# One weight split, one convolution and one pair of evictions moved inside a hybrid DeltaNet and attention layer

## The chip, the cores and the metric

The kernel runs on one core of a Trainium2 chip. The metric is the device time of one execution in microseconds (us), the median of the runs shown. TensorE is PE in the profile (its weight loads are PEld), VectorE is DVE, ScalarE is ACT, GpSimd is POOL, and SyncE, which issues the DMAs, is SP.

## The reference

One layer of a flow-matching backbone handles 512 latent tokens and 128 context tokens of width 1024 with shared weights. Everything is float32.

```python
h = modulate(rmsnorm(x), shift1, scale1)          # shifts, scales: silu(cond) @ w_ada
u = h @ w_in                                      # q, k, v, z, beta and decay logits, NA q/k/v, gates
qkv = silu(short_conv(qkv, conv_w))               # 3 taps along the tokens
o_dn = gated_delta(l2norm(q), l2norm(k), v, g, beta)   # both directions, 8 heads, chunked
o_na = softmax(q_na @ k_na + bias) @ v_na         # 8 heads, 8 x 16 window plus the context keys
x = x + gate1 * ((sig(gA) * (o_dn @ w_pa) + sig(gB) * (o_na @ w_pb)) @ w_out)
x = x + gate2 * swiglu(modulate(rmsnorm(x), shift2, scale2))
```

## The kernel before

Activations lie feature-major: 1024 features are 8 blocks `k` of 128 partitions, and the 640 tokens lie along the free axis. A PSUM bank holds 512 floats, so a product over 640 tokens goes to two banks as two halves of 320 tokens (`HALVES`). Exact float32 products are made from two rounded parts: an operand is split into `big` (rounded, written by ACT) and `small` (the rest, a subtraction on DVE), and each block takes three products (big by big, big by small, small by big), each in two halves: six matmuls of 128x320. The orders on all five engines are written out by hand; the engines meet only at semaphores (`e.wait_ge`) and at named steps (`Steps`), and each engine works strictly in its written order.

**Opening.** Four groups of `w_ada` columns (`ada_group`, four loads each, the third group into tile WAH, the fourth into wa_last) give the shifts and scales of two feature blocks each. ACT copies each group's sums out, PE turns them (`ada_select`), and DVE makes the gains (`gains(p)`, L2618 to L2623). DVE multiplies the input by the inverse norm (`normed`, L2608), applies the gain (`exact_h`, L2630), ACT rounds it (`round_h`) and DVE subtracts (`small_h`, L2636). In the same stretch DVE splits three weights: `opening_kind("q", 1)`, `opening_kind("k", 2)` and that of the beta and decay logits, `wbas`, all by `opening_small` (L2591). PE goes through pairs of blocks `p`: an ada group, the q product, the select, the k product (L1282), and then `logits_mm` (L1298 and L1300), whose first call waits for the logits' split (`pro_lo` 3).

**Heads.** Eight DeltaNet heads follow, each about 77 us. A head ends with a scan of five steps over the tiles, in both directions at once. In step `s` PE makes `ks` (L1537), DVE makes `r` (L2901), PE makes `y` (L1544), ACT scales it, PE makes `av` (L1555, L1556), and DVE updates the state `S` (L2913, not in steps 0 and 4) and adds the output `o` (L2918). PE puts blocks of dense products between these. On DVE `CONV_AT[s]` names the pieces of the next head's convolution that run in step `s`: the first tuple after `r` and before `S`, the second after `o`. Each of q, k and v has three pieces, 0, 1 and the last (L2685, L2688, L2691), each a pass over 641 columns. In step 4, before `o`, DVE also makes the small part of the next dense weight (`small("6")`, L2784), which PE's products right after the last `av` need. The head ends with normalising `o` (L2942), a turn of it on PE (`turn o`, L1588), and the next head's first products. The last head makes no convolution.

**Attention.** Twenty rounds `j` of two (head, tile) units each are interleaved with 56 blocks `pa_block(n, k)` of `o_dn @ w_pa` (L1604), eight for each of the output groups n = 1 to 7 (group 0 is done before with another form). All groups use the same two PSUM banks, 6 and 7. `pa_evict(n)` on DVE (L2993, two instructions of 320 tokens) multiplies the sums by the gate. The last block of group n-1, the scores of the next round (L1645, L1647) and the first block of group n stand in this order on PE; the first block waits for `pa_out`, which the second instruction of the eviction raises. On DVE the eviction stands behind the two `-max` instructions (L3021) of the round and before the two `P` scalings (L3027, L3030).

After these come `w_pb`, `w_out` and the feed-forward part (L1850), which the diff does not touch.

Of the kernel before, what the change touches and what calls it, by code (L numbers as in the profile page):

```python
# [10 lines left out]
ALU = mybir.AluOpType  # L11
# [5 lines left out]
KD = D // P  # L17
# [141 lines left out]
    return STRIPS[part][SPLIT[part].index(at) + 1] if at in SPLIT[part] else None  # L159


CONV_AT = {0: (("q0",), ("q1",)), 1: (("q",), ("k0",)), 2: (("k1",), ("k",)), 3: (("v0",), ("v1",)), 4: (("v",), ())}


def dve_steps():
# [243 lines left out]
def build(nc, A):  # L409
    top = ExitStack()  # L410
    with top:
# [3 lines left out]
        def sem(name):  # L415
            return top.enter_context(nc.semaphore(name))
# [16 lines left out]
        xT, h_small = sb_rounded("xT", [P, KD, TOK])  # L433
        oT, oT_r = sb_rounded("oT", [P, H, TOK])
        naT, naT_r = sb_rounded("naT", [P, KP, TOK])
        W, W_r = sb_rounded("W", [P, 4, KD, P])
        ps = top.enter_context(nc.psum_tensor("ps", [P, 8, 512], F32))
# [38 lines left out]
        xn_done = sem("xn_done")  # L476
# [73 lines left out]

        ld_pa = [sem(f"ld_pa{i}") for i in range(2)]
        pa_mm = sem("pa_mm")
        pa_read = sem("pa_read")
        pa_out = sem("pa_out")
        oT_hi = sem("oT_hi")
# [51 lines left out]
        start = work.enter_context(ExitStack())  # L607
        xin = sb("xin", [P, NT, D], start)
        xs = sb("xs", [P, KD, TOK], start)
        rows = sb("rows", [P, 2, P], start)  # L610
        sqx = sb("sqx", [P, 2, TOK], start)
        rstd = sb("rstd", [P, TOK], start)
        wba = sb("wba", [P, KD, 4 * H], start)
        wbas = sb("wbas", [P, KD, 2, 4 * H], start, F32R)
# [5 lines left out]
        xn = xinf.rearrange("p (k c) -> p k c", k=KD)  # L620
# [76 lines left out]
        pa_big = sb("pa_big", [P, 2, KD, P], na, F32R)  # L697
# [6 lines left out]
        pa_slot, pa_small = ([w[:, i, :, :] for i in (2, 3)] for w in (W, W_r))  # L704
# [108 lines left out]
        HALVES = ((0, HT), (HT, HT))  # L813
# [413 lines left out]
        def _(e):  # L1227
# [4 lines left out]
            for t in range(NT):  # L1232
                e.wait_ge(ld_x[t], 16)
                for j in range(2):
                    n = 2 * t + j
# [361 lines left out]
            def wait(steps, name):  # L1597
                e.wait_ge(steps.sem, steps.after(name))

            def three(bank, big, small, x_big, x_small, k, k_n):  # L1600

                for i, (w, x) in enumerate(((big, x_big), (big, x_small), (small, x_big))):
                    for b, (a, n) in enumerate(HALVES):
                        m = e.matmul(ps[:, bank + b, 0:n], w[:, k, :], x[:, k, a:a + n], start=k == 0 and i == 0, stop=k == k_n - 1 and i == 2, skip_group_check=True)  # L1604
                return m

            def pa_block(n, k):

                if k == 0:
                    if n:  # L1610
                        e.wait_ge(pa_lo, n)
                    else:
                        e.wait_ge(ld_pa[0], 16)
                    e.wait_ge(pa_out, n)
                if n == 0 and k == KD - 1:
                    e.wait_ge(dve_dn.sem, dve_dn.value(H - 1, "o out"))
                if n == 0:
                    for b, (a, w) in enumerate(HALVES):
                        m = e.matmul(ps[:, 6 + b, 0:w], pa_slot[0][:, k, :], oT[:, k, a:a + w], start=k == 0, stop=k == KD - 1, skip_group_check=True)
                    m.then_inc(pa_read, 1)  # L1620
                else:
                    if n == 1:
                        e.wait_ge(oT_lo, k + 1)
                    m = three(6, pa_big[:, n % 2, :, :], pa_small[n % 2], h_small, oT_r, k, KD)
                    if k == KD - 1:
                        m.then_inc(pa_mm, 1)

            def shared(slot):
# [950 lines left out]
        def _(e):  # L2579
# [8 lines left out]
            def opening_small(w_r, w, big, n):  # L2588

                e.wait_ge(pro_hi, n)  # L2590
                e.tensor_tensor(w_r, w, big, ALU.subtract).then_inc(pro_lo, 1)  # L2591

            def opening_kind(kind, n):

                opening_small(W_r[:, slot[kind], :, :], W[:, slot[kind], :, :], OPENING_BIG[kind], n)
# [6 lines left out]
                e.tensor_scalar(diag[:, t, :], IDN, cols[:, SSQ + t:SSQ + t + 1], None, ALU.mult).then_inc(diag_done, 1)  # L2602
            e.wait_ge(rstd_done, 2)
            e.wait_ge(x_out, 2 * NT)
            def normed(p):

                for k in (2 * p, 2 * p + 1):
                    e.tensor_tensor(xn[:, k, :], xs[:, k, :], rstd[:, :], ALU.mult).then_inc(xn_done, 1)  # L2608

            def gains(p):  # L2610

# [21 lines left out]
            def small_h(k):  # L2633

                e.wait_ge(h_round, k + 1)
                e.tensor_tensor(h_small[:, k, :], xn[:, k, :], h_big[:, k, :], ALU.subtract).then_inc(h_done, 1)  # L2636

            normed(0)
            normed(1)
            e.wait_ge(vec_out, 1)  # L2640
            gains(0)
            exact_h(0)
# [1 line left out]
            small_h(0)  # L2644
            exact_h(1)
            small_h(1)
            opening_kind("k", 2)
            gains(1)
            exact_h(2)
            exact_h(3)  # L2650
            small_h(2)
            small_h(3)
            opening_small(wbas[:, :, 1, :], wba[:, :, :], wbas[:, :, 0, :], 3)
            normed(2)
            normed(3)
            gains(2)
            exact_h(4)
            exact_h(5)
# [326 lines left out]

            def pa_evict(n):
                e.wait_ge(ld_gate[n % 2], 16 * (n // 2 + 1))
                if n:
                    e.wait_ge(pa_mm, n)
                else:  # L2990
                    e.wait_ge(pa_read, KD)
                for b, (a, w) in enumerate(HALVES):
                    m = e.scalar_tensor_tensor(hT[:, n, a:a + w], tA[:, n % 2, a:a + w], 1.0, ps[:, 6 + b, 0:w], ALU.add, ALU.mult)  # L2993
                m.then_inc(pa_out, 1)

            def na_lo_of(p):
# [533 lines left out]
```

## Time and profile before

| what | value |
|---|---|
| median of 3 runs | 1338.67 us (1338.6 to 1339.28) |
| the profiled execution, its own time | 1338.55 us |
| its span, first to last instruction | 1336.8 us |
| PE busy | 1309.7 us (98%) |
| DVE, ACT, POOL busy | 71%, 52%, 13% |
| mean granted TensorE clock | 0.993 |

The span is 1.75 us below the time of the same execution; the rest lies around it. A busy PE is modelled: a matmul of 320 columns is shown with about 0.31 us, but in a dense stretch the next starts 0.147 us later. A short wait of PE therefore shows less in its idle time than in the distance between starts.

### The profile page before, as it was taken

To read this page: it belongs to the slowest core of one execution; us is meant where nothing else is said; L and a number is where in the kernel's file an instruction comes from. 1 tells how busy PE (TensorE), PEld (TensorE's weight loads), DVE (VectorE), ACT (ScalarE), POOL (GpSimd) and SP (SyncE) were. 2 spreads that over 40 slices of the span, in tenths; PEclk is the share of its full clock that TensorE was granted. 3 is DMA by queue.
4 is the path that set the end of the run, shared out by engine and by line. 5 is a ranking of instruction groups with operands and counts; after the bars stand their busy time and mean duration, and the time that the engine had idled before them with its cause. 6 is when DMAs were issued, how large, how long until landed. Compare 5 with 4: busy or idle time off the path is not lost.

```text
span 1336.8 us, 25932 instructions
## 1 busy us (share of the span) xinstructions
PE 1309.7 (98%) x9818; PEld 1221.2 (91%) x9818; DVE 954.3 (71%) x2212; ACT 700.6 (52%) x1578; POOL 171.3 (13%) x161
## 2 busy tenths in 40 slices
PE   6999999999999999999999999999999999999998
PEld 4798899999999989999997888999999999999998
DVE  5666766767676776767536566757999788987995
ACT  4463645456373645546356554437564355534643
POOL 1002020200102020100122220000102300041022
PEclk7999999999999999999999999999999999999999
DMA  9653533323233333314517223622232233233223
GB/s 315 213 141 95 160 100 117 89 82 112 86 113 100 117 94 113 100 31 120 155 54 230 72 70 109 208 63 64 64 95 79 80 96 95 64 95 95 74 62 104
DMA packets 207860, 144.59 MB, mean 108 GB/s; under 512 B 9471, under 2 KB 197159, under 8 KB 207607
## 3 DMA queue, kind: packets, MB, share of 16 engines
q1 hardware_dynamic: 207447, 142.79, 36.4%
q8 instruction: 79, 1.29, 0.4%
q14 instruction: 46, 0.38, 0.1%
q10 hardware_dynamic: 288, 0.13, 0.0%
HBM read 126.73 MB, written 17.99 MB: 108 GB/s over the span
## 4 chain that ended last, share of the span: by engine, by line
PE 85%; DVE 9%; issue 3%; ACT 2%; DMA 1%; SPq 1%; POOL 0%; DVEq 0%; POOLq 0%; ACTq 0%
PE ps L1282 31%; PE ps L1850 22%; PE ps L1604 8%; PE ps L1736 2%; PE ps L1537 2%; PE ps L1477 2%; PE ps L1256 2%; PE ps L1471 1%; PE ps L1449 1%; PE ps L1544 1%; PE ps L1704 1%; PE ps L1556 1%; PE ps L1555 1%; PE ps L1690 1%; PE ps L1645 1%
## 5 line engine op out<-in xcount | busy, mean ns | idle before, releaser
L1282 PE MATMUL ps<-hT_r,WAH_r 128*128 128x320 f32 x912 | 226.4, 329 | 1.3 <-DVE P6c L2831 0.4
L1282 PE MATMUL ps<-xT_r,WAH_r 128*128 128x320 f32 x912 | 208.0, 309 | 0.0
L1282 PEld LDWEIGHTS ps<-hT_r,WAH_r 128*128 128x128 f32 x912 | 147.6, 189 | 19.1 <-issue 14.4
L1282 PEld LDWEIGHTS ps<-xT_r,WAH_r 128*128 128x128 f32 x912 | 153.4, 189 | 0.0
L1850 PE MATMUL ps<-d_part_r,W_r 128*128 128x320 f32 x660 | 136.9, 310 | 1.5 <-DVE xT L3269 1.0
L1282 PE MATMUL ps<-hT_r,W_r 128*128 128x320 f32 x592 | 134.6, 310 | 0.0
L1850 PEld LDWEIGHTS ps<-d_part_r,W_r 128*128 128x128 f32 x660 | 107.5, 188 | 2.9 <-DVE xT L3269 2.2
L1850 PE MATMUL ps<-t_big_r,W_r 128*128 128x320 f32 x380 | 107.5, 310 | 1.4 <-DVE c L3245 1.4
L1850 PE MATMUL ps<-b_part,W_r 128*128 128x320 f32 x456 | 101.2, 309 | 0.0
L1282 PEld LDWEIGHTS ps<-hT_r,W_r 128*128 128x128 f32 x592 | 99.6, 190 | 0.1
L1850 PE MATMUL ps<-t_small_r,W_r 128*128 128x320 f32 x304 | 93.9, 309 | 0.0
L1282 PE MATMUL ps<-hT_r,naT_r 128*128 128x320 f32 x400 | 91.9, 311 | 0.8 <-DVE xT_r L2636 0.8
L3441 POOL TENSOR_TENSOR gm<-sqkq,dt 128x1280 f32<-128x1280 f32 x8 | 23.5, 2933 | 522.7 <-DVE Xc L2840 522.7
L1850 PEld LDWEIGHTS ps<-b_part,W_r 128*128 128x128 f32 x456 | 76.3, 188 | 0.0
L1282 PEld LDWEIGHTS ps<-hT_r,naT_r 128*128 128x128 f32 x400 | 67.0, 189 | 6.2 <-DVE xT_r L2636 3.7
L3495 POOL TENSOR_TENSOR oT<-oT 128x512 f32<-128x512 f32 (+1 forms) x12 | 19.5, 1629 | 411.6 <-PE ps L1850 281.0
L1850 PEld LDWEIGHTS ps<-t_big_r,W_r 128*128 128x128 f32 x380 | 69.0, 188 | 2.4 <-DVE c L3245 2.1
L3269 DVE SCALAR_TENSOR_TENSOR xT<-ps,mods,xT 128x192 f32<-128x192 f32 (+2 forms) x132 | 51.0, 423 | 21.8 <-PE ps L1850 21.3
L2400 ACT ACTIVATE W_r<-oT 128x512 fp32r<-128x512 f32 (+1 forms) x101 | 61.0, 607 | 7.4 <-PE ps L1850 7.3
L1850 PEld LDWEIGHTS ps<-t_small_r,W_r 128*128 128x128 f32 x304 | 57.1, 188 | 0.0
L2192 ACT ACTIVATE tq<-ps,prm 128x128 f32<-128x128 f32 x64 | 20.7, 365 | 66.4 <-DVE rv L2901 59.4
L2409 ACT ACTIVATE W_r<-w_more 128x512 fp32r<-128x512 f32 (+1 forms) x62 | 36.9, 610 | 34.3 <-POOL w_more L3500 21.3
(459 smaller groups left out, 3276.3 us busy)
## 6 DMA issues: line engine op xcount, KB each, us to landing
oT<-in_ffn_w SPq DMA_DIRECT2D x44, 512.0 KB, 5.2
W<-in_w_in SPq DMA_DIRECT2D x36, 512.0 KB, 4.6
WAH<-in_w_ada SPq DMA_DIRECT2D x16, 1024.0 KB, 6.9
naT<-in_w_in SPq DMA_DIRECT2D x24, 512.0 KB, 4.3
ext_dram<-naT SPq DMA_DIRECT2D x28, 320.0 KB, 4.2
oT<-in_ffn_w SPq DMA_DIRECT2D x32, 256.0 KB, 3.8
tA<-ext_dram SPq DMA_DIRECT2D x16, 320.0 KB, 4.0
GCB<-gc_dram SPq DMA_DIRECT2D x7, 640.0 KB, 4.3
```

Source lines behind the costliest of these rows:

```text
L1256: m = e.matmul(ps[32 * j:32 * j + 32, bank, 0:n], csT[:, k, :], w[:, k, :], start=k < 4, stop=k >= 4, skip_group_check=True)
L1282: m = e.matmul(ps[:, bank + b, 0:n], w[:, k, :], x[:, k, a:a + n], start=k == 0 and i == 0, stop=k == KD - 1 and i == 2, skip_group_check= ...
L1477: m = e.matmul(ps[g:g + 32, 5, r:r + P], one[:, u, :], other[:, u, :], start=True, stop=True, skip_group_check=True)
L1537: m = e.matmul(ps[:, 2 + d, w * P:(w + 1) * P], kq[:, tile[d], w, :], S[:, d, :], start=True, stop=True, skip_group_check=True)
L1604: m = e.matmul(ps[:, bank + b, 0:n], w[:, k, :], x[:, k, a:a + n], start=k == 0 and i == 0, stop=k == k_n - 1 and i == 2, skip_group_check ...
L1736: m = e.matmul(ps[:, PB_BANKS[n % 3] + b, 0:c], w, x[:, a:a + c], start=k == 0 and i == 0, stop=k == KP - 1 and i == 2, skip_group_check=True)
L1850: m = e.matmul(ps[:, bank, 0:HT], w[i][:, k, :], x[i][:, k, :], start=start and k == 0 and j == 0, stop=k == half - 1 and j == 2, skip_gro ...
L2192: act_dn.done(e.activation(tq[:, d, :], ps[:, 2 + d, P:2 * P], ACT.Copy, scale=prm[:, EG, u:u + 1]), f"qs {s} {'fb'[d]}")
L2400: act_ff.done(e.activation(w_big[i][:, 0:tiles_half(p), :], raw_half(p, s, j), ACT.Copy), f"{o} {p}")
L2409: act_ff.done(e.activation(w_big[i][:, 0:half, :], w_small_f[i][:, 0:half, :], ACT.Copy), f"{o} {p}")
L3269: m = e.scalar_tensor_tensor(x, ps[:, bank, a - half * HT:a - half * HT + w], mods[:, 2 * g + s + 40, c:c + 1], x, ALU.mult, ALU.add)
L3441: pool_dn.done(e.tensor_tensor(typed(AT[:, :, :]), kqs[:, :, 1, :].unsqueeze(1).to_broadcast([P, 2, NT, P]), typed(dtm[:, :, :]), ALU.mult ...
```

## The change

Three edits, all of order or of when a semaphore is raised; no arithmetic is added or removed.

1. Opening, on DVE: `normed` now takes one block instead of two. Its block 4 goes ahead of the k split, the logits' split goes to right behind the k split, block 5 behind that, and blocks 6 and 7 to where 4 to 7 stood.
2. Heads, on DVE: v's piece 1 moves from after `o` in step 3 to right behind piece 0 in the same step, before `S`; v's last piece moves from step 4 to after `o` in step 3.
3. Attention: in the last block (k = 7) and the first block (k = 0) of each group, PE makes the three products of the first 320 tokens and then the three of the last 320. A new semaphore is raised after the first half of the last block (`pa_half`) and another after the first instruction of an eviction (`pa_half_out`). The eviction's first instruction waits for the first half alone, and the next group's first half waits for that instruction alone, its second half for the whole eviction. Group 1's first block still waits for the whole eviction of group 0.

```diff
-CONV_AT = {0: (("q0",), ("q1",)), 1: (("q",), ("k0",)), 2: (("k1",), ("k",)), 3: (("v0",), ("v1",)), 4: (("v",), ())}
+CONV_AT = {0: (("q0",), ("q1",)), 1: (("q",), ("k0",)), 2: (("k1",), ("k",)), 3: (("v0", "v1"), ("v",)), 4: ((), ())}
...
+            def three_of(b, bank, big, small, x_big, x_small, k, k_n):
+
+                a, n = HALVES[b]
+                for i, (w, x) in enumerate(((big, x_big), (big, x_small), (small, x_big))):
+                    m = e.matmul(ps[:, bank + b, 0:n], w[:, k, :], x[:, k, a:a + n], start=k == 0 and i == 0, stop=k == k_n - 1 and i == 2, skip_group_check=True)
+                return m
...
-                    e.wait_ge(pa_out, n)
+                    e.wait_ge(pa_half_out if n > 1 else pa_out, n)
...
-                    m = three(6, pa_big[:, n % 2, :, :], pa_small[n % 2], h_small, oT_r, k, KD)
-                    if k == KD - 1:
+                    own = 6, pa_big[:, n % 2, :, :], pa_small[n % 2], h_small, oT_r, k, KD
+                    if 0 < k < KD - 1:
+                        three(*own)
+                        return
+                    m = three_of(0, *own)
+                    if k:
+                        m.then_inc(pa_half, 1)
+                    else:
+                        e.wait_ge(pa_out, n)
+                    m = three_of(1, *own)
+                    if k:
                         m.then_inc(pa_mm, 1)
...
-            normed(0)
-            normed(1)
+            for k in range(KD // 2):
+                normed(k)
             e.wait_ge(vec_out, 1)
...
             small_h(1)
+            normed(4)
             opening_kind("k", 2)
+            opening_small(wbas[:, :, 1, :], wba[:, :, :], wbas[:, :, 0, :], 3)
+            normed(5)
             gains(1)
             exact_h(2)
             exact_h(3)
             small_h(2)
             small_h(3)
-            opening_small(wbas[:, :, 1, :], wba[:, :, :], wbas[:, :, 0, :], 3)
-            normed(2)
-            normed(3)
+            normed(6)
+            normed(7)
             gains(2)
...
                 for b, (a, w) in enumerate(HALVES):
+                    if n:
+                        e.wait_ge((pa_half, pa_mm)[b], n)
                     m = e.scalar_tensor_tensor(hT[:, n, a:a + w], tA[:, n % 2, a:a + w], 1.0, ps[:, 6 + b, 0:w], ALU.add, ALU.mult)
+                    if not b:
+                        m.then_inc(pa_half_out, 1)
                 m.then_inc(pa_out, 1)
```

## Rows read from the trace of the kernel before

**Rows 1.** The page: busy time of each engine.

```profile
PE 1309.7 (98%) x9818; PEld 1221.2 (91%) x9818; DVE 954.3 (71%) x2212; ACT 700.6 (52%) x1578; POOL 171.3 (13%) x161
```

**Rows 2.** Waits of PE and PEld: line, releaser, us in total, times, longest.

```profile
PE ps L1604 <- DVE hT L2993: 1.3, 3, 0.7
...
PEld ps L1282 <- DVE naT_r L2784: 2.1, 7, 0.3
```

**Rows 3.** Timeline of the opening: start, us, engine line op, idle before.

```profile
28.44 1.23 DVE L2591 TENSOR_TENSOR W_r<-W,oT_r 128x1024 fp32r<-128x1024 f32 x1 [1.07 <-ACT oT_r L1967]
...
29.48 0.41 ACT L1967 ACTIVATE wbas<-wba 128x256 fp32r<-128x256 f32 x1
...
31.65 0.26 DVE L2618 TENSOR_REDUCE mods<-ps 128x4 f32<-128x16 f32 x2 [1.98 <-PE ps L1275]
...
32.91 0.46 PE L1282 MATMUL ps<-hT_r,W_r 128*128 128x320 f32 x2
...
35.43 0.42 DVE L2591 TENSOR_TENSOR wbas<-wba,wbas 128x256 fp32r<-128x256 f32 x1
35.76 3.03 DVE L2608 TENSOR_TENSOR xin<-xs,rstd 128x640 f32<-128x640 f32 x4
...
35.90 0.50 PE L1298 MATMUL ps<-hT_r,wbas 128*64 128x320 f32 x2 [2.53 <-DVE wbas L2591]
...
37.21 1.92 PE L1256 MATMUL ps<-WAH,csT 128*32 128x512 f32 x16
...
41.57 0.26 DVE L2618 TENSOR_REDUCE mods<-ps 128x4 f32<-128x16 f32 x2 [2.78 <-PE ps L1275]
```

**Rows 4.** Tile WAH, opening: its DMA issues and their landing.

```profile
L901 SPq DMA_DIRECT2D WAH<-in_w_ada x4: 509/1444/2714, 22.6 to 28.4; - x4
...
DMA to landing us min/median/max: 6.4/6.4/7.1
```

**Rows 5.** Timeline of head 2, steps 3 and 4 of its scan.

```profile
291.48 0.55 DVE L2685 TENSOR_SCALAR conv<-raws,taps 128x641 f32<-128x641 f32 x1
...
293.48 0.79 DVE L2913 SCALAR_TENSOR_TENSOR S<-S,prm,ps 128x128 f32<-128x128 f32 x2 [1.45 <-PE ps L1556]
...
295.90 0.88 DVE L2691 SCALAR_TENSOR_TENSOR conv<-raws,taps,conv 128x641 f32<-128x641 f32 x1
...
296.70 1.22 DVE L2784 TENSOR_TENSOR naT_r<-naT,WAH_r 128x1024 fp32r<-128x1024 f32 x1
...
297.97 0.30 PEld L1282 LDWEIGHTS ps<-hT_r,WAH_r 128*128 128x128 f32 x2 [0.30 <-DVE naT_r L2784]
```

**Rows 6.** Timeline of the end of head 2.

```profile
304.75 0.83 DVE L2942 TENSOR_TENSOR ob<-ob,orn 128x640 f32<-128x640 f32 x1
...
305.98 0.71 PE L1588 MATMUL ps<-sq_c,ob 128*128 128x128 f32 x5
```

**Rows 7.** Timeline of attention: scores, then a block of w_pa; evictions.

```profile
711.62 0.39 PE L1647 MATMUL ps<-ckT,WAH 64*128 64x128 f32 x4
...
711.94 0.56 PE L1604 MATMUL ps<-xT_r,pa_big 128*128 128x320 f32 x2
...
723.90 0.39 PE L1647 MATMUL ps<-ckT,WAH 64*128 64x128 f32 x4
...
724.57 0.53 PE L1604 MATMUL ps<-xT_r,pa_big 128*128 128x320 f32 x2 [0.29 <-DVE hT L2993]
...
757.98 0.89 DVE L2993 SCALAR_TENSOR_TENSOR hT<-tA,ps 128x320 f32<-128x320 f32 x2 [0.70 <-PE ps L1604]
...
759.02 0.53 PE L1604 MATMUL ps<-xT_r,pa_big 128*128 128x320 f32 x2 [0.72 <-DVE hT L2993]
...
807.97 0.39 PE L1647 MATMUL ps<-ckT,WAH 64*128 64x128 f32 x4
...
808.64 0.53 PE L1604 MATMUL ps<-xT_r,pa_big 128*128 128x320 f32 x2 [0.28 <-DVE hT L2993]
```

**Rows 8.** One microsecond of the end of the opening; the 0.50 is PE's clock.

```profile
76.00:77.00 1.00, 1.00 (x6) 1.00 (x5) 0.00 (x0) 1.00 (x1) 0.00 (x0) 0.50 0.77 145
```

More of the change, by code:

```diff
@@ L552, in build @@
         pa_mm = sem("pa_mm")
+        pa_half = sem("pa_half")
+        pa_half_out = sem("pa_half_out")
         pa_read = sem("pa_read")
@@ L2604, in _, with normed @@
             e.wait_ge(x_out, 2 * NT)
-            def normed(p):
-                for k in (2 * p, 2 * p + 1):
-                    e.tensor_tensor(xn[:, k, :], xs[:, k, :], rstd[:, :], ALU.mult).then_inc(xn_done, 1)
+            def normed(k):
+                e.tensor_tensor(xn[:, k, :], xs[:, k, :], rstd[:, :], ALU.mult).then_inc(xn_done, 1)
             def gains(p):
@@ L2987, in pa_evict @@
                 e.wait_ge(ld_gate[n % 2], 16 * (n // 2 + 1))
-                if n:
-                    e.wait_ge(pa_mm, n)
-                else:
+                if not n:
                     e.wait_ge(pa_read, KD)
                 for b, (a, w) in enumerate(HALVES):
+                    if n:
+                        e.wait_ge((pa_half, pa_mm)[b], n)
                     m = e.scalar_tensor_tensor(hT[:, n, a:a + w], tA[:, n % 2, a:a + w], 1.0, ps[:, 6 + b, 0:w], ALU.add, ALU.mult)
+                    if not b:
+                        m.then_inc(pa_half_out, 1)
                 m.then_inc(pa_out, 1)
```

## The prediction

> **What bounds the kernel now.** I began with the page. PE is busy for 1309.7 of 1336.8 us [rows 1], so only 27.1 us of the whole span can be won without taking work from PE, and any edit is worth what it takes out of PE's own stream of starts. The second view is the list of waits of PE and of its weight loads. It shows few waits in the stages touched here: for the eviction L2993, and for the small weight part L2784, seven times 0.3 us, once in each head but the last [rows 2]. The third is the timeline at each of those places, which says what PE could have started and when. It also shows the longest of these waits, 2.53 us for the logits' split in the opening [rows 3]. Because PE's busy time is modelled, I read distances between starts there, not idle time.
>
> **Opening.** PE's last matmul pair before the wait starts at 32.91 and the next may follow 2 x 0.147 = 0.29 us later, at 33.20; the logits start at 35.90 [rows 3]. So 2.70 us are at stake. The reason is DVE's order alone: ACT had the big part at 29.48 + 0.41 = 29.89, and DVE subtracted at 35.43 behind a gain that itself waited for PE until 31.65 [rows 3].
>
> New order on DVE. One `normed` costs 3.03 / 4 = 0.76 us. Block 4 goes into the 1.07 us that DVE stood waiting ahead of 28.44, so the k split stays at 28.44 to 29.67. The logits' split can begin at about 29.95 and ends at 30.37 (0.42 us), and block 5 ends at 31.13, before the gains can start at 31.65 [rows 3]. All added work is thus covered by two idle stretches; without the first cover the k split would be up to 0.76 us late, ending at 30.43, before PE's k product needs it. The split is 2.8 us early at 33.20. Blocks 6 and 7 keep their place and now end 1.5 us earlier; DVE waited 2.78 us for PE after them anyway [rows 3].
>
> What is late next: the third ada group, which started at 37.21, 1.31 us after the logits, and would start at 34.51. Its second half starts some 0.93 us on, at 35.4, and needs the last WAH load. That was issued at 28.4 and landings took 6.4 to 7.1 us, so it is there between 34.8 and 35.5 [rows 3, 4]. Cost between 0 and 0.1 us; if other loads hold it up, 0.5. No load is issued anew or moved on SP's queue before 43 us, and the rest of the opening follows PE, so I take 2.65 us, with ends 2.1 and 2.7.
>
> **Heads.** After the last `av` PE's weight loads wait 0.30 us for L2784, which ends at 296.70 + 1.22 = 297.92 [rows 5]. Ahead of it stands v's last piece, 0.88 us from 295.90. With that piece gone the subtraction can start at 295.90 and ends at 297.12; the loads could go at 297.67. The wait goes, seven times, 2.1 us in total [rows 2, 5].
>
> Does the moved piece 1 cost anything in step 3? DVE was idle for 1.45 us ahead of `S` at 293.48. Piece 0 runs from 291.48 for 0.55; piece 1 follows after the 0.1 us that a wait for one's own result takes and runs 0.88 us, to 293.05. It fits with 0.43 us to spare, so `S` and PE's next `ks` are not late [rows 5]. After `o` of step 3 the last piece (0.88) takes the place of piece 1 (0.88), so `r` of step 4 comes when it did. Nothing on POOL or SP moves.
>
> Later in the head PE reaches `turn o` 0.30 us sooner. Its input ends at 304.75 + 0.83 = 305.58 and PE came at 305.98 [rows 6]. That input hangs on an ACT chain that the edit does not shift, so at most 0.33 to 0.40 us can be kept per head. 0.30 to 0.36 fits just under it. I take 7 x 0.32 = 2.25 us; ends 1.4 (if the chain to `turn o` takes 0.1 us of each) and 2.5.
>
> **Attention.** A block of `w_pa` that waits for nothing starts 0.32 us after the last score group (711.62 to 711.94). At the first block of a group it is 0.67 us (723.90 to 724.57), so 0.35 are lost; at the last of the six places, n = 7, again 0.67 (807.97 to 808.64); at n = 4, where the scores are short, the wait is 0.72 [rows 7]. The three others lost 0.15, 0.15 and 0.19 by the same reading. The sum is 1.9 us, of which the list of waits shows 1.3 [rows 2].
>
> How much of it goes? One eviction instruction takes 0.44 to 0.48 us, half of 0.89. At n = 4 the first half of the sums is complete three matmuls (0.44 us) before 757.87, so DVE starts at 757.54 rather than 757.98 and is free of bank 6 at 758.02. PE can begin at 758.2, as the scores end, where it began at 759.02 [rows 7]. Its second half starts at 758.64 and needs the second instruction, which ends at 758.50: just in time. At the other places the margin is larger. The scalings of `P` behind the eviction come some 0.4 us sooner, as PE does. At n = 6 DVE is busy until 792.36 and wins only 0.1, but PE loses only 0.19 there. The matmuls are as many as before; three in a row into one bank is what the feed-forward part does at the same 0.147 us. The second wait inside a block is one that is mostly over when PE comes: nothing to 0.05 us each, seven times. I take 1.8 us; ends 0.8 (the 1.3 shown less 0.5 for new waits) and 2.0.
>
> **Sum.** 2.65 + 2.25 + 1.8 = 6.7 us. On the profiled execution's own time, 1338.55, that is 1331.85, its span 1330.1; that execution is 0.12 below the median of the runs, so from 1338.67 I forecast 1332.0 us. The ends of the three sum to 4.3 and 7.2 us: 1331.5 to 1334.4.
>
> **The clock.** The rows show PE's granted clock at 0.50, which is 1.2 instead of 2.4 GHz, in 76 to 77 us [rows 8], about 3.3 us in all, right after the stretch of small matmuls that closes the opening. At half clock pairs of matmuls start 0.53 instead of 0.29 us apart, so this stretch costs about 3.3 x 0.24 / 0.53 = 1.5 us. These small matmuls now come 2.7 us earlier. The clock may then not fall, or fall for twice as long.
>
> The Trainium skill, in "TensorE: Matmul & The Clock Gate", Part 1, says that the window over which activity is watched is free-running and does not start with the kernel. By that rule the same stream of matmuls can meet the gate otherwise from one execution to the next and the change would add or take 1.5 us without being its cause. The spread of the three runs, 0.7 us, neither shows nor excludes this.
>
> **Rivals.**
> - *All three gains, clock as before* (the forecast): 1332.0. Chance 0.55.
> - *The clock falls otherwise at the end of the opening.* For: the pieces move against whatever the gate looks at. Against: the same matmuls in the same order. 1330.5 without the low stretch (chance 0.12), 1333.5 with a doubled one (0.10).
> - *Part of the gain is not there.* The freed PE meets a next wait: WAH in the opening (0.5), `turn o` in the heads (0.8 to 2.2), `P` or the second half in attention (1.0). For: the margins of 0.1 at three places. Against: each was computed as met. 1334.4, chance 0.17.
> - *The opening edit does not do what it says*, because DVE's subtraction is held by something that the trace hides behind its old order: 1334.7, chance 0.03.
> - *Slower than before: `S` of step 3 is late.* Place: between `r` and `S` in seven heads. Price: PE's next `ks` waits on `S` directly, so every microsecond of delay costs seven. It decides when piece 1 delays `S` by more than 6.7 / 7 = 0.96 us, and shows as slower when by more than 1.34 us, that is when piece 1 ends at 294.8 or later instead of 293.05. Piece 1 would have to take or wait 1.75 us more than the 0.88 shown [rows 5]; its input was copied in step 0. Chance 0.03.
>
> **Range and chances.** What this kernel's measurement can tell from no change is about 0.2%, 2.7 us. The range runs from the clock's good case with full gains, 1329.8, to the lost gains with some of the clock's bad case, 1335.0. Faster by over 0.2% (below 1336.0) holds in all cases but the last and the worst of the partial ones: 0.94; same 0.04; slower 0.02.
>
> **What the profile after would show.** Right: no wait of PE for `wbas`, the logits at 33.2 and the third group at 34.5; no wait for L2784 in the seven heads, and `S` of step 3 still preceded by some 0.4 us of idle DVE; first blocks of L1604 0.32 us behind the scores at five places. A head would be 76.3 us long instead of 76.65. Wrong: a new wait for DMA of WAH; PE or PEld waiting at L1588 for L2942; L1690 waiting for L3030 at n = 4; a clock row of 0.50 at another place or for longer.

## The result and the profile after

The changed kernel takes 1330.12 us (median of 6 runs, 1329.61 to 1332.81), the kernel before in the same session 1338.8 (6 runs, 1336.24 to 1340.27): ratio 0.9941, 95% interval 0.9928 to 0.9954. (The ratio is estimated from all runs and is nearer to that of the means, a difference of 7.9 us; the two medians alone differ by 8.7.) Forecast were 1332.0 us and a range of 1329.8 to 1335.0. The profiled execution took 1330.0 us with a span of 1328.2, which is 8.6 us less than before; the three edits had been summed to 6.7.

From the page after, the row that answers [rows 1]; and of the windows after, one microsecond that answers [rows 8] (the last three figures: PE's clock, DMA share, GB/s):

```profile
PE 1306.0 (98%) x9818; PEld 1218.1 (92%) x9818; DVE 957.9 (72%) x2212; ACT 700.6 (53%) x1578; POOL 170.8 (13%) x161
```

```profile
76.00:77.00 1.00, 1.00 (x8) 0.97 (x7) 0.00 (x0) 0.16 (x1) 0.00 (x0) 1.00 1.04 280
```

The instruction counts are the same. PE's modelled busy time fell by 3.7 us, though no edit takes matmuls away: the stretch at half clock, gone here, is a part of it.

The timeline of the opening after, for [rows 3]:

```profile
26.74 0.82 DVE L2625 TENSOR_TENSOR xin<-xs,rstd 128x640 f32<-128x640 f32 x1
28.05 1.23 DVE L2609 TENSOR_TENSOR W_r<-W,oT_r 128x1024 fp32r<-128x1024 f32 x1 [0.49 <-ACT oT_r L1985]
...
29.37 0.42 DVE L2609 TENSOR_TENSOR wbas<-wba,wbas 128x256 fp32r<-128x256 f32 x1
29.71 0.82 DVE L2625 TENSOR_TENSOR xin<-xs,rstd 128x640 f32<-128x640 f32 x1
30.79 0.26 DVE L2635 TENSOR_REDUCE mods<-ps 128x4 f32<-128x16 f32 x2 [0.26 <-PE ps L1277]
...
32.34 0.45 PE L1300 MATMUL ps<-hT_r,wbas 128*64 128x320 f32 x2
...
33.60 2.13 PE L1258 MATMUL ps<-WAH,csT 128*32 128x512 f32 x16
...
34.66 0.16 PEld L1258 LDWEIGHTS ps<-WAH,csT 128*32 128x32 f32 x8 [0.91 <-DMA WAH<-in_w_ada]
```

The k split, the logits' split, block 5 and the gains follow each other as forecast, and the logits start without a wait. The last line is new: the second half of the third ada group now waits for the last load of WAH. The group takes 2.13 instead of 1.92 us.

Head 2 after, for [rows 5, 6]:

```profile
285.78 0.54 DVE L2704 TENSOR_SCALAR conv<-raws,taps 128x641 f32<-128x641 f32 x1
286.36 0.89 DVE L2707 SCALAR_TENSOR_TENSOR conv<-raws,taps,conv 128x641 f32<-128x641 f32 x1
287.76 0.79 DVE L2932 SCALAR_TENSOR_TENSOR S<-S,prm,ps 128x128 f32<-128x128 f32 x2 [0.52 <-PE ps L1558]
...
288.87 0.88 DVE L2710 SCALAR_TENSOR_TENSOR conv<-raws,taps,conv 128x641 f32<-128x641 f32 x1
289.67 0.60 DVE L2920 SCALAR_TENSOR_TENSOR rv<-ps,prm,vrow 128x128 f32<-128x128 f32 x2
290.19 1.22 DVE L2803 TENSOR_TENSOR naT_r<-naT,WAH_r 128x1024 fp32r<-128x1024 f32 x1
...
299.04 0.82 DVE L2961 TENSOR_TENSOR ob<-ob,orn 128x640 f32<-128x640 f32 x1
...
299.57 0.46 PE L1284 MATMUL ps<-hT_r,naT_r 128*128 128x320 f32 x2
300.01 0.74 PE L1590 MATMUL ps<-sq_c,ob 128*128 128x128 f32 x5
```

DVE is still idle for 0.52 us ahead of `S` (0.43 forecast), and L2803 follows `r` directly. `turn o` starts 0.44 us after the last pair, where a pair that nothing holds is followed after 0.29: 0.15 us of a new small wait, since its input ends at 299.86. But this is so in head 2 alone. In the other six heads `turn o` follows unheld, as in head 3:

```profile
375.18 0.83 DVE L2961 TENSOR_TENSOR ob<-ob,orn 128x640 f32<-128x640 f32 x1
...
376.00 0.46 PE L1284 MATMUL ps<-hT_r,naT_r 128*128 128x320 f32 x2
...
376.29 0.71 PE L1590 MATMUL ps<-sq_c,ob 128*128 128x128 f32 x5
```

Attention after, n = 4, for the 0.72 us of [rows 7] (scores, first block, eviction):

```profile
750.05 0.49 PE L1665 MATMUL ps<-WAH 64*128 64x128 f32 x4
750.47 0.41 PE L1606 MATMUL ps<-xT_r,pa_big 128*128 128x320 f32 x1
...
751.02 0.31 PE L1606 MATMUL ps<-xT_r,pa_big 128*128 128x320 f32 x1
```

```profile
749.79 0.88 DVE L3012 SCALAR_TENSOR_TENSOR hT<-tA,ps 128x320 f32<-128x320 f32 x2 [0.27 <-PE ps L1606]
```

The first block starts 0.42 us behind the scores instead of 1.22, and the eviction began before the scores did. At n = 2, 3, 5 and 7 it is 0.32 us and at n = 6 0.35, where 0.32 had been forecast for five places.

### The profile page after: what moved, and what is told of

The parts are those of the page before. It is cut to its first block, busy times and chain, and to the rows that moved or that the text cites. A ratio compares the mean times of both kernels' runs of the same rounds, so it can differ in the third digit from the quotient of the medians.

```text
span 1328.2 us, 25930 instructions
## 1 busy us (share of the span) xinstructions
PE 1306.0 (98%) x9818; PEld 1218.1 (92%) x9818; DVE 957.9 (72%) x2212; ACT 700.6 (53%) x1578; POOL 170.8 (13%) x161
## 3 DMA queue, kind: packets, MB, share of 16 engines
q8 instruction: 79, 1.29, 0.4%
## 4 chain that ended last, share of the span: by engine, by line
PE 86%; DVE 8%; ACT 2%; issue 2%; DMA 1%; SPq 1%; POOL 0%; DVEq 0%; POOLq 0%; ACTq 0%
PE ps L1284 31%; PE ps L1868 22%; PE ps L1613 7%; PE ps L1539 3%; PE ps L1754 2%; PE ps L1479 2%; PE ps L1258 2%; PE ps L1546 2%; PE ps L1473 2%; PE ps L1451 1%; PE ps L1558 1%; PE ps L1722 1%; PE ps L1606 1%; PE ps L1557 1%; PE ps L1708 1%
## 5 line engine op out<-in xcount | busy, mean ns | idle before, releaser
L1868 PEld LDWEIGHTS ps<-b_part,W_r 128*128 128x128 f32 x456 | 76.2, 188 | 0.0
```

The costliest lines, as they stand in the source:

```text
L1868: m = e.matmul(ps[:, bank, 0:HT], w[i][:, k, :], x[i][:, k, :], start=start and k == 0 and j == 0, stop=k == half - 1 and j == 2, skip_gro ...
```

## The experiments

All fourteen profiles read in one way, by distances between starts of PE: the first matmul of head 0 (L1451 of the changed kernel, `kq`), the same of head 7, the first of `w_out` (L1613, `y_big`), the last turn (L1927). The first three kernels are the kernel before, three times; all3, after and after2 are the changed kernel. o_only, h_only and a_only have one edit each; the others are explained where they come up. "Low" says whether a second stretch at granted clock 0.50 stands near the end of the opening.

| kernel | head 0 starts | low | seven heads | head 7 to w_out | w_out to last turn |
|---|---|---|---|---|---|
| before | 81.59 | 75.8 to 79.2 | 531.71 | 237.81 | 479.43 |
| none | 81.07 | 74.6 to 78.0 | 531.67 | 237.82 | 479.60 |
| none2 | 81.16 | 74.8 to 78.3 | 531.76 | 237.79 | 479.75 |
| o_only | 76.59 | no | 531.71 | 238.55 | 479.55 |
| h_only | 80.64 | 74.6 to 78.0 | 529.20 | 238.78 | 479.79 |
| a_only | 81.72 | 76 to 79.4 | 531.70 | 235.98 | 479.59 |
| all3 | 76.90 | no | 529.24 | 236.10 | 479.90 |
| after | 76.64 | no | 529.21 | 236.14 | 479.99 |
| after2 | 78.10 | 72.3 to 75.7 | 529.23 | 236.35 | 479.94 |
| s_late | 78.48 | 71.9 to 75.3 | 529.89 | 236.54 | 479.69 |
| half_last | 78.23 | 72.8 to 76.2 | 529.20 | 236.89 | 479.92 |
| half_first | 77.05 | no | 529.23 | 237.91 | 479.58 |
| s_late_y | 76.88 | no | 528.56 | 236.49 | 479.68 |
| conv_y | 76.53 | no | 526.60 | 237.02 | 479.95 |

The stage of the seven heads repeats to 0.1 us in one code, the others to 0.5 or 1 us.

### Each edit alone, and all three

The kernel before with one edit each (the diffs are the three parts of the one above), and the changed kernel again.

> The opening edit alone on the kernel before; nothing of the computation is left out. Theory A (three independent waits of PE, and a clock that falls or not by chance): the first logits matmul starts 2.7 us earlier relative to the first h block, and the median is 2.7 us below that of before (ratio 0.998). Whether the low-clock stretch near the end of the opening is there is open under this theory and worth 1.5 us in one profile. Theory B (the opening edit itself removes the low-clock stretch, as the profile of the changed kernel has none there): about 4.2 us (ratio 0.9969), no granted clock under 1 between 68 and 82 us. Theory C (a later wait eats it): under 1 us.

> The heads edit alone: v's convolution a piece sooner. Theory A: 0.36 us per head between the starts of two heads' first matmuls, 7 heads, 2.5 us (ratio 0.9981). Theory C (turn o takes back what the ACT chain does not follow): 0.20 us a head, 1.4 us. S of step 3 still behind 0.5 us of idle DVE.

> The attention edit alone. Theory A: from the first eviction to the first w_out matmul 1.7 to 1.8 us less, ratio 0.9987. Theory C (waits in the middle of a block or on P give it back): under 0.9 us.

> The changed kernel itself beside its three parts on the same chip. Theory A: the sum of the three parts, 6.9 us (ratio 0.9948), to within 0.5. If the parts interact, or the clock goes with the opening edit (theory B), more than their sum: 8.4 us.

Measured against 1338.11 us for the kernel before on the same chip (27 runs): opening alone 1334.95 (11 runs, ratio 0.9976, 0.9967 to 0.9985); heads alone 1336.04 (11 runs, 0.9988, 0.9979 to 0.9996); attention alone 1336.38 (11 runs, 0.9989, 0.998 to 0.9998); all three 1330.19 (5 runs, 0.9944, 0.9931 to 0.9956). Each interval lies below 1, but none decides between its theories: the opening's 0.9976 lies between A (0.998) and B (0.9969), and the 7.5 us of all three lie between A (6.9) and B (8.4).

The table gives the sizes more sharply. Heads alone: 531.71 - 529.20 = 2.51 us in the seven heads. Attention alone: 237.81 - 235.98 = 1.83 us. Attention alone leaves the heads' column as it was, and all3 keeps both gains. Heads alone has 0.97 us more in the column of attention; 0.48 of that is a late load (below) and 0.38 lies at the first block of n = 7, where the eviction started 0.92 us after the last pair of the last block instead of 0.56, for a reason that was not found. It is not there in all3 or after. Theory A holds for both edits. The opening alone shows two things beside its missing stall: its second ada half waited longer than in the changed kernel, and the low stretch was absent.

```profile
31.36 0.45 PE L1298 MATMUL ps<-hT_r,wbas 128*64 128x320 f32 x2
...
34.62 1.07 PE L1256 MATMUL ps<-WAH,csT 128*32 128x512 f32 x8 [0.93 <-DMA WAH<-in_w_ada]
```

Its timeline above (PE alone) shows PE a microsecond early at the logits, because the granted clock was back at 1.00 at 25.2 us instead of 30 or 31. The wait for the load took that microsecond.

### Both kernels once more: the clock and the load

The kernels before and after, unchanged, one profile each.

> The kernel before once more, for the granted clock. Three profiles with the old opening (before, and heads or attention alone) showed a stretch of 3.5 us at half clock that begins 2.9 to 3.2 us after the start of the 20 one-column matmuls that close the opening; three with the new opening did not. Theory B (the clock falls there because of where the old opening puts this stretch): low at 75 to 79 us again. Theory of chance: one in two that it is absent.

> The kernel before once more, for the low-clock stretch at the end of the opening. Four of four profiles with the old opening showed it, two of six with the new one. If the old opening brings it: low at 74 to 79 us, first kq at 80.6 to 81.7 us. If it is chance: one in three to one in two that it is absent, with the first kq at 79.2 to 80 us and 1.6 us less in all.

> The changed kernel once more, for the same stretch and for the landing of the last piece of WAH. If its landing bounds the opening: the second half of the third ada group starts at 34.6 to 35.1 us whatever the clock did before 30 us, and the first kq is at 76.5 to 76.9 us without the low stretch, 78.2 to 78.5 with it.

They took 1338.16, 1338.47 and 1331.63 us. One microsecond of the windows of none2, then of after2, then of all3 (the same columns as above):

```profile
76.00:77.00 1.00, 1.00 (x6) 1.00 (x5) 0.00 (x0) 0.99 (x3) 0.00 (x0) 0.50 0.86 264
```

```profile
74.00:75.00 1.00, 1.00 (x6) 1.00 (x5) 0.73 (x4) 0.00 (x0) 0.00 (x0) 0.50 0.92 274
```

```profile
74.00:75.00 1.00, 1.00 (x9) 1.00 (x8) 0.52 (x3) 0.31 (x2) 0.00 (x0) 1.00 0.77 289
```

The clock is granted at 0.50 (1.2 GHz) or 1.00 (2.4 GHz), and PE is busy all the time in both cases. With the old opening the low stretch stood in all five profiles, with the new one in three of nine (after2, s_late, half_last). So the new opening does not exclude it: theory B of the run o_only is refuted. If old and new had the same odds, five of the eight low profiles in fourteen would all fall on the old ones in 56 of 2002 ways, 2.8%.

The runs without a profile speak against so sharp a difference. Of the 27 runs of the kernel before, 16 list a mean granted clock of 0.993 or 0.994 and take 1337.79 to 1339.67 us; 11 list 0.995 to 0.998 and take 1334.94 to 1337.01. Two of these, both of 1334.94 us, list 0.998. That leaves room for at most 2 x 0.0025 x 1333.1 = 6.7 us at half clock, less than two stretches of 3.41 us, the shortest seen. So the old opening has executions without the second stretch too, if they had a first one as every profile has. Whether its odds differ at all from those of the new one is open. In the eight profiles that show it, the second stretch begins 2.4 to 3.6 us after the start of the same burst of 20 one-column matmuls, which stands in both openings.

In after2 the clock was back at 28 us, and the load took what PE had won:

```profile
32.25 1.06 PE L1258 MATMUL ps<-WAH,csT 128*32 128x512 f32 x8
...
34.61 1.07 PE L1258 MATMUL ps<-WAH,csT 128*32 128x512 f32 x8 [1.29 <-DMA WAH<-in_w_ada]
```

PE waits here 1.29 us. Over the nine profiles with the new opening this second half starts at 34.6 to 35.1, whenever PE came; in eight PE waited for the load, in s_late PE came last, at 35.01. From there to head 0 it is 41.97 us in five of them without the low stretch (34.62 to 76.59, 34.93 to 76.90, 34.56 to 76.53, 34.91 to 76.88; 35.09 to 77.05 is 41.96), and 43.49 in two with it (34.61 to 78.10, 34.74 to 78.23). Two results: in eight of nine profiles the last piece of WAH now sets the end of the opening, and the low stretch costs 43.49 - 41.97 = 1.52 us. DMA is busy there; of the windows after,

```profile
33.00:36.00 3.00, 3.00 (x23) 0.92 (x22) 2.91 (x5) 1.05 (x3) 0.00 (x0) 1.00 1.10 347
```

its share is 1.10 at 347 GB/s while the last pieces land. Whether another order of the loads would bring this one sooner was not tried.

### Which half of the attention edit

Two kernels undo one half each. half_last leaves the first block of a group unsplit and lets it wait for the whole eviction; half_first leaves the last block unsplit, so that both instructions of the eviction wait for all sums.

```diff
 half_last, against the changed kernel
-                    e.wait_ge(pa_half_out if n > 1 else pa_out, n)
+                    e.wait_ge(pa_out, n)
...
-                    if 0 < k < KD - 1:
+                    if k < KD - 1:
...
 half_first, against the changed kernel
-                    m = three_of(0, *own)
-                    if k:
-                        m.then_inc(pa_half, 1)
-                    else:
-                        e.wait_ge(pa_out, n)
-                    m = three_of(1, *own)
...
+                    if k:
+                        m = three(*own)
...
-                        e.wait_ge((pa_half, pa_mm)[b], n)
+                        e.wait_ge(pa_mm, n)
```

> The changed kernel with the first block of w_pa of each group unsplit again and waiting for the whole eviction; the last block stays split, so that DVE's eviction still begins after the first half of the sums. Theory A (what counts is that the eviction ends 0.4 us sooner): PE waits only where it had waited by more than 0.4 us, at n = 4 by about 0.3, so 0.1 to 0.5 us slower than the changed kernel, 1330.2 to 1330.6. Theory B (the split of the first block, which lets PE start on one bank, does most of it): 0.8 to 1.4 us slower, 1331 to 1331.6, and first blocks 0.5 to 0.6 us behind the scores again.

> The changed kernel with the last block of each group unsplit again, so that both halves of DVE's eviction start only after the whole group's sums; the first block stays split. Read by starts of PE between the first matmul of head 7 and the first of w_out: 237.8 us before, 236.1 with the whole attention edit, 236.9 with the last block split alone (half of that run's loss was a wait elsewhere; 0.55 us lay at the blocks themselves). If the two halves of the edit add up: the first block's split is worth 0.5 to 0.6 us, so 237.2 to 237.3. If either alone brings most: 236.5 to 236.7.

half_last: 1331.74 us (5 runs, 1330.23 to 1332.31; ratio to before 0.9947, 0.9933 to 0.996), half_first one run of 1331.82. Their PE timelines at n = 4, half_first first, then half_last:

```profile
751.40 0.49 PE L1662 MATMUL ps<-WAH 64*128 64x128 f32 x4
752.21 0.39 PE L1606 MATMUL ps<-xT_r,pa_big 128*128 128x320 f32 x1 [0.32 <-DVE hT L3009]
```

```profile
751.63 0.49 PE L1662 MATMUL ps<-WAH 64*128 64x128 f32 x4
752.40 0.53 PE L1613 MATMUL ps<-xT_r,pa_big 128*128 128x320 f32 x2 [0.28 <-DVE hT L3009]
```

Scores to first block: 1.22 us before, 0.81 with the first block split alone, 0.77 with the last alone, 0.42 with both. At n = 7 these are 0.67, 0.63, 0.59 and 0.32. At the four other places (n = 2, 3, 5, 6) either half of the edit alone gives the 0.32 to 0.35 us of both together. So one half would have done at four of the six places, and only n = 4 and n = 7 need both. Set beside the changed kernel matmul by matmul, half_last falls back by 0.55 us in all at the blocks, half_first by 0.70 at the two and by 0.2 in small steps elsewhere. Of the 1.83 us of the whole, the last block's split alone keeps 1.28 and the first block's alone about 1.1; the two do not add up. The 0.55 lie between the two theories of half_last, whose medians were both too low (1331.74 came, with the low stretch in its profile). half_first lies outside both forecasts with 237.91 us, by the rest of its longer stage, which is this (PE):

```profile
708.53 1.12 PE L1683 MATMUL ps<-sqn,sq_c 128*128 128x512 f32 x2 [0.57 <-ACT sqn L2350]
```

ACT's `sqn` waited for a load of `feats`. Over the fourteen profiles `sqn` started 8.7 to 10.4 us after the issue of the first load of `feats`, and in the six where that was 9.9 or more PE lost 0.3 to 0.8 us. That explains the 238.55 of o_only and half of the 238.78 of h_only.

### What a late S costs

s_late puts v's last piece ahead of `S` as well:

```diff
-CONV_AT = {0: (("q0",), ("q1",)), 1: (("q",), ("k0",)), 2: (("k1",), ("k",)), 3: (("v0", "v1"), ("v",)), 4: ((), ())}
+CONV_AT = {0: (("q0",), ("q1",)), 1: (("q",), ("k0",)), 2: (("k1",), ("k",)), 3: (("v0", "v1", "v"), ()), 4: ((), ())}
```

> The changed kernel with one difference: all three pieces of v's convolution stand ahead of S in step 3 of every head. The last piece takes 0.88 us and, after v1, it ends some 0.36 us after S could otherwise have begun plus the 0.1 us of the wait for one's own result, so S starts 0.45 to 0.55 us later than in the changed kernel (its idle 0.52 us ahead of S is used up first). Theory of the prediction (the price per us of delay of S in step 3 is one us per head, seven or eight heads): head period 76.3 + 0.5 = 76.8 us, the kernel 3 to 4.5 us slower than the changed one, 1333.5 to 1334.5. Rival (PE has other work to put in S's place, or o and r come no later): at most 1 us slower, 1330 to 1331.

It took 1331.45 us (4 runs, 1329.88 to 1332.62; ratio to before 0.9946, 0.9932 to 0.996), 2 us short of the prediction's theory and 0.45 above the rival's range. Its PE timeline in head 2:

```profile
290.58 1.16 PE L1539 MATMUL ps<-S,kq 128*128 128x128 f32 x8 [0.30 <-DVE S L2932]
...
292.46 0.61 PE L1546 MATMUL ps<-rv,XT 128*128 128x128 f32 x4
```

The wait came, 0.30 us in each of seven heads, but the heads grew by only (529.89 - 529.22) / 7 = 0.10 us. The second line shows part of why: PE's `y` of step 4 (L1546) took 0.75 us in the changed kernel, 0.61 here, because `r` no longer stands behind a piece of 0.88 us. Of the 0.31 us lost at `S`, 0.16 come back there. In five heads that is all, and they are 0.12 to 0.17 us longer. In this head the small wait at `turn o` goes as well, and in head 4 `y` gives back 0.33; these two are as long as in the changed kernel. So the edit had left a small cost at `r`, and that suggested two more kernels:

```diff
 conv_y
-CONV_AT = {0: (("q0",), ("q1",)), 1: (("q",), ("k0",)), 2: (("k1",), ("k",)), 3: (("v0", "v1"), ("v",)), 4: ((), ())}
+CONV_AT = {0: (("q0", "q1"), ("q",)), 1: (("k0", "k1"), ()), 2: (("k", "v0"), ()), 3: (("v1",), ()), 4: ((), ("v",))}
 s_late_y
+CONV_AT = {0: (("q0", "q1"), ("q",)), 1: (("k0", "k1", "k"), ()), 2: (("v0", "v1"), ()), 3: (("v",), ()), 4: ((), ())}
```

> The changed kernel with the pieces of the convolution spread otherwise: q wholly in step 0, k0 and k1 ahead of S in step 1, k and v0 ahead of S in step 2, v1 ahead of S in step 3, v behind o in step 4, so that v's last piece lies ahead of the final weight part again but r of steps 3 and 4 has nothing new ahead of it. If r and the part L2803 set the end of a head: either the wait of 0.3 us per head for L2803 returns (2 us slower, 1332 to 1332.5), or, if two pieces of 0.55 and 0.88 us behind each other ahead of S make S late in any of steps 0 to 2, more (0.3 to 1 us per head, up to 1337). If the order only shortens the waits of r: up to 2 us faster than the changed kernel, 1328 to 1330.

> The price of a late S by itself: the kernel conv_y with k's three pieces ahead of S in step 1 (v0 and v1 ahead of S in step 2, v in step 3), and no piece of the convolution behind any o but q, so that nothing gives the delay back. In conv_y DVE stood idle for 0.55 us ahead of S in step 1; the added piece takes 0.88 us, so S is 0.33 to 0.38 us late and PE's next ks 0.25 to 0.35. Price of one us per us and head: the head 75.95 + 0.3 = 76.25 us, 2.1 us over seven heads. If PE's later work in the head takes the delay up: 75.95 to 76.05 us.

s_late_y took 1329.63 us in one run. Its timeline in step 1 of head 2:

```profile
277.20 0.55 DVE L2704 TENSOR_SCALAR conv<-raws,taps 128x641 f32<-128x641 f32 x1
277.78 0.89 DVE L2707 SCALAR_TENSOR_TENSOR conv<-raws,taps,conv 128x641 f32<-128x641 f32 x1
278.70 0.89 DVE L2710 SCALAR_TENSOR_TENSOR conv<-raws,taps,conv 128x641 f32<-128x641 f32 x1
279.51 0.60 DVE L2932 SCALAR_TENSOR_TENSOR S<-S,prm,ps 128x128 f32<-128x128 f32 x2
...
279.90 1.16 PE L1539 MATMUL ps<-S,kq 128*128 128x128 f32 x8 [0.28 <-DVE S L2932]
```

`S` has no idle time ahead of it. Counted from the head's first matmul it is 0.28 us later than in conv_y (55.23 instead of 54.95), PE waits 0.28 us, and the heads are (528.56 - 526.60) / 7 = 0.28 us longer. A full head is 76.23 us, 76.25 forecast. With nothing to give it back, the price is one for one.

### A better order

conv_y took 1328.12 us (5 runs, 1327.29 to 1329.02; ratio to before 0.9922, 0.9909 to 0.9934), 2.0 us less than the changed kernel by medians of different sessions, where the two intervals still touch. The heads' column is the surer measure. Its head 2, step 4 and end:

```profile
287.98 0.80 DVE L2920 SCALAR_TENSOR_TENSOR rv<-ps,prm,vrow 128x128 f32<-128x128 f32 x2
288.69 1.22 DVE L2803 TENSOR_TENSOR naT_r<-naT,WAH_r 128x1024 fp32r<-128x1024 f32 x1
...
289.11 0.61 PE L1546 MATMUL ps<-rv,XT 128*128 128x128 f32 x4
...
291.29 0.88 DVE L2710 SCALAR_TENSOR_TENSOR conv<-raws,taps,conv 128x641 f32<-128x641 f32 x1
...
297.65 0.83 DVE L2961 TENSOR_TENSOR ob<-ob,orn 128x640 f32<-128x640 f32 x1
...
298.79 0.71 PE L1590 MATMUL ps<-sq_c,ob 128*128 128x128 f32 x5
```

Against the changed kernel, in head 2, PE wins 0.15 us at `y` of step 3, 0.15 at `y` of step 4 and 0.13 at `turn o`; in the heads whose `turn o` was not held, `y` alone gives 0.31. A full head is 75.95 us long, and the seven 526.60 instead of 529.21. The wait of 0.3 us for L2803 does not return, since v's last piece now stands behind it. It is the fastest version that was run. Its next stage gave back 0.9 us, about 0.4 of it at a late `feats` and 0.6 later, at a wait of 0.5 us for `yB`. after2, half_last and s_late_y also lost 0.2 us there; whether conv_y's 0.6 is chance was not settled.

## Why the prediction was right, point by point

**The sum.** The three edits were forecast at 2.65, 2.25 and 1.8 us; measured are 2.8, 2.5 and 1.7 to 1.8.

**Opening.** In the profiled pair head 0 starts 4.95 us earlier. 0.86 of that is there before the edit acts (last pair ahead of the logits at 32.05 instead of 32.91); 2.70 is the stall, exactly the 2.70 at stake; 1.39 lies behind the logits, where the low stretch is missing (1.52) and the third group with its wait for WAH takes 0.15 more (3.32 instead of 3.17 us from the logits to the next product). The 0.86 and the 1.52 belong to the clock and the execution, not to the edit. In the mean, the start of head 0, with 1.52 us taken off where the stretch is low, is 79.60 in before, none, none2 and h_only (a_only, with one more low stretch, left out) and 76.76 in the nine with the new opening: 2.8 us for the edit. In all four of the old, the first low stretch ended late, at 30.2 us or after; the four of the new that share this (all3, after, s_late, s_late_y) give 2.75. The step that was undersized is the cost of the next thing that is late. It was priced at 0 to 0.1 us (0.5 if other loads held it up). WAH made PE wait in eight of nine profiles, by 0.1 to 1.4 us, because PE can reach it 1.35 us sooner when the clock rises early (32.25 in after2, 33.60 in after), and the load does not come sooner. It caps the opening: the five in which the clock was back by 28 us start head 0 hardly sooner (76.69 in the mean) than the four others (76.85). In such an execution the edit should be worth about a microsecond less than 2.75, an estimate from the logits (31.0 to 31.8 there, 32.3 to 32.9 in the four); no profile of the old opening shows the case.

**Heads.** The wait for L2803 is gone and `S` was not late, as said. Set beside the kernel before matmul by matmul, each head gains 0.35 to 0.39 us at the first matmuls behind that weight part and nothing anywhere else; taken had been 0.32, from the 0.30 us that PEld is shown idle. The limit at `turn o`, by which the prediction justified its number, was not there in six of seven heads. It had been read in head 2, where PE came 0.40 us behind the input; in the others that was 0.57 to 0.68, and they keep all of their gain. Head 2 alone lost 0.17 of it at `turn o` and kept 0.25. So the total of 2.5 us is close, and the 0.36 in the mean lies in the 0.33 to 0.40 of that limit by coincidence. A head is 76.33 us in the mean of heads 1 to 6, 76.3 forecast. What the prediction did not see is that a piece of 0.88 us after `o` delays `r`, and PE's `y` behind it, by 0.15 us. It wrote that `r` of step 4 comes when it did; that is true, and it was late before too.

**Attention.** 1.83 us alone and 1.67 in the changed kernel, against 1.8. In the changed kernel another 0.14 us were lost ahead of the blocks at L1473; h_only shows the same loss and s_late does not, so it goes with the heads edit. The gains lie at the six first blocks and nowhere else: 0.36, 0.13, 0.76, 0.11, 0.15 and 0.32 us for n = 2 to 7 in a_only. No wait for the second instruction of an eviction was seen, and splitting a block into two runs of three costs nothing that shows: from the block's first matmul to the next group's it is the same.

**The slower rival.** A late `S` was priced at one for one, seven times over. s_late_y shows that price (0.28 for 0.28). s_late shows that an order can give half of it back in the same head, and all of it in two heads. It never came near the 0.96 us from which it would have decided.

**The clock.** This rival did occur, on the good side, given a chance of 0.12: 1330.5 us without the low stretch was its number, and 1330.12 was measured. Its price, 1.5 us, was right to 0.02. Its odds are not known: the stretch was absent in six of nine profiles of the new opening and in none of five of the old. If all runs weigh it so, 6/9 x 1.52 = 1.0 us of the difference is the clock's, and 2.8 + 2.5 + 1.75 + 1.0 less about 0.35 in the feed-forward part is 7.7 us, beside the measured 1338.8 x 0.0059 = 7.9 (6.2 to 9.6). But the runs without a profile make the five old profiles a doubtful sample, so this 1.0 is a guess and not a size. At like granted clock, beside the parts, nine runs before (0.995 and 0.996, median 1336.28 us) stand 6.3 us above three of all3 (1329.94 to 1330.19), and the two of 0.998 stand 4.7 above its one (1330.28). That is near the 6.7 that had been summed, with few runs. The forecast missed 1.9 us of the 8.7 between the medians. The terms of the sum were 0.3 to 0.4 us too low; the rest is not assigned with certainty. The clock is the only difference seen that is large enough, and how it falls in six runs is chance, so where the median came to lie in the range, near its lower end, is in part luck. The Trainium skill, "TensorE: Matmul & The Clock Gate", Part 1, says that the activity window is free-running and does not start with the kernel. Runs agree in so far as one program shows both: after and all3 without the stretch, after2 with it. Why all five profiles of the old opening met it, that rule does not say.

**The feed-forward part.** It was to be unchanged. From the first of `w_out` to the last turn it took 0.56 us more in the pair. Over the fourteen it is 479.43 to 479.99 us: 479.59 in the mean of the three profiles of the kernel before and 479.94 in the three of the changed one, but 479.58 to 479.69 in half_first, s_late and s_late_y, which have the same opening. Whether the 0.35 us is real was not settled.

## What to carry to other kernels

When a stall is taken away, look for the load behind it: here every execution in which PE came early ended at the same landing time, so the next gain in the opening is to be looked for in DMA order or volume and not in DVE's order (not tried). On an engine that serves a chain, ask not only whether a filler piece is done in time but also which chain member stands behind it: putting fillers ahead of the member that waits for PE anyway (`S`) and not ahead of the one that PE waits for (`r`) won as much again in the heads (2.6 us) as the edit had (2.5). Read a margin in every repeat of a stage and not in one: the head that was read was the only one in which `turn o` was near. And measure by distances between starts inside the trace: the seven heads repeat to 0.1 us, where medians of whole runs carried 1.5 us of clock and up to 0.8 us of load latency.

## What the runs showed of the hardware

- The same program's second low-clock stretch came or stayed away from execution to execution (in after2, not in after or all3). It was 3.4 us long in all eight profiles that show it, with PE busy in the microseconds shown, and cost 1.52 us where profiles with and without it could be set side by side.
- The first low stretch, in the opening, began between 16.6 and 21.8 us and ended between 25.0 and 31.4 us over the fourteen profiles. Ahead of it PE had stood waiting for loads (in after, busy for 2.51 of 4.5 us from 12 to 16.5 us, and the clock fell at 16.6). A 2.5 to 3.2 us wait of PE at 31 to 36 us was not followed by a fall in four of five profiles of the old opening; in a_only it was, from 35.0 to 38.4 us.
- On an otherwise steady schedule one load (`feats`) was late in six profiles, by up to 1.7 us against the earliest, and cost PE up to 0.8 us.
